# A fifth weight chunk's products ordered by hand among the gates and the first tile of a chunked recurrence

## What is computed

```python
proj = einsum("bsd,de->bse", rms_norm(x, attn_norm), w_in)        # 1024 x 4104
q_a, k_a, v_a, g_a, beta_a, alpha_a, q_b, k_b, v_b, g_b = split(proj)
# a: gated delta rule, 4 heads of 128, after a causal convolution of q_a, k_a, v_a and silu
beta = sigmoid(beta_a);  g = -exp(a_log) * softplus(alpha_a + dt_bias);  gc = cumsum(g)
# per chunk of tokens: (I + A) u = rhs is solved, then
v_new = u - w @ state;  o = q_dec @ state + attn @ v_new;  state = state * last + k_dec^T @ v_new
# b: retention, 4 heads of 128, rotary q and k, the same kind of state recurrence
x = x + concat(o_a, o_b) @ w_out
x = x + top-2 mixture of 64 experts(rms_norm(x, ffn_norm))
return rms_norm(x, final_norm)
```

## Time and profile before

| | |
|---|---|
| median of three runs | 2205.02 us |
| the profiled execution's own time | 2204.05 us |
| its span, first to last instruction | 2202.3 us |
| what lies around the span | 1.75 us |
| busy shares of the span: PE, DVE, ACT, POOL | 88%, 37%, 28%, 23% |
| mean granted TensorE clock | 0.946 of full |

### The profile page before, as it was taken

How to read it: one execution, slowest core, us unless ns; L and a number is a source line. 1 busy time by engine, 2 the same in 40 slices (tenths; PEclk the granted TensorE clock), 3 DMA queues, 4 the chain that set the end, 5 groups by cost and what they waited for, 6 DMA issues and landing times. The chain is left out here.

```text
span 2202.3 us, 30297 instructions
## 1 busy us (share of the span) xinstructions
PE 1939.9 (88%) x11659; PEld 1334.3 (61%) x11659; DVE 814.9 (37%) x1457; ACT 622.2 (28%) x1325; POOL 514.4 (23%) x587
## 2 busy tenths in 40 slices
PE   5999999999899989999998589999969887888880
PEld 5998866666687766878887566766633232332220
DVE  5223245555433542440110446766631111111115
ACT  4333145555323442331210333322212111111111
POOL 2235240000120110001111577666311111111103
PEclk9999999999999999999999699999969998999895
DMA  5113461211321154722321512221468999999986
GB/s 191 50 40 123 143 204 25 49 25 44 125 77 39 42 112 68 94 57 94 91 86 59 191 64 92 78 88 54 170 264 360 424 424 425 423 421 420 418 359 241
DMA packets 101711, 371.75 MB, mean 169 GB/s; under 512 B 17413, under 2 KB 40138, under 8 KB 74698
## 3 DMA queue, kind: packets, MB, share of 16 engines
q1 hardware_dynamic: 83722, 323.59, 41.0%
q0 software_dynamic: 16704, 42.10, 4.9%
q10 hardware_dynamic: 1152, 4.19, 0.5%
HBM read 321.47 MB, written 65.14 MB: 176 GB/s over the span
## 5 line engine op out<-in xcount | busy, mean ns | idle before, releaser
L2712 PE MATMUL ps<-w_gu,rows_t 128*64 128x512 f32 x1024 | 263.7, 674 | 62.8 <-DMA w_gu<-w_up 61.1
L2712 PEld LDWEIGHTS ps<-w_gu,rows_t 128*64 128x64 f32 x1024 | 79.9, 154 | 223.5 <-issue 158.3
L930 PE MATMUL ps<-k_s,q_s 96*128 96x512 f32 (+3 forms) x384 | 150.7, 503 | 0.0
L2787 DVE TENSOR_TENSOR act_s<-act_g,ps 128x256 f32<-128x256 f32 x32 | 13.5, 421 | 334.2 <-ACT act_g L2778 334.2
L2970 POOL DMA_INDIRECT y_d<-y_out,asg_i x32 | 32.1, 1004 | 438.0 <-DVE y_out L2796 438.0
L305 PE MATMUL ps<-tk_lo,h_hi 128*128 128x512 f32 x320 | 125.4, 392 | 3.0 <-DVE tk_lo L297 3.0
L305 PE MATMUL ps<-tk_hi,h_lo 128*128 128x512 f32 x320 | 125.1, 391 | 0.0
L305 PE MATMUL ps<-tk_hi,h_hi 128*128 128x512 f32 x320 | 125.1, 391 | 0.0
L2185 PE MATMUL ps<-w_o,mix_t 128*128 128x512 f32 x256 | 124.8, 616 | 0.0
L2730 PE MATMUL ps<-w_d,act_tt 128*64 128x512 f32 x512 | 116.9, 598 | 0.5 <-issue 0.5
L484 PE MATMUL ps<-w_u_lo,x_hi 128*128 128x444 f32 (+2 forms) x256 | 93.7, 366 | 15.4 <-DVE x_lo L297 15.4
(11 more groups left out here) (447 smaller groups left out, 3995.6 us busy)
## 6 DMA issues: line engine op xcount, KB each, us to landing
w_gu<-w_gate SPq DMA_DIRECT2D x64, 1024.0 KB, 22.1
w_gu<-w_up SPq DMA_DIRECT2D x64, 1024.0 KB, 25.5
w_d<-w_down SPq DMA_DIRECT2D x64, 1024.0 KB, 19.0
w_tk<-w_in SPq DMA_DIRECT2D x5, 2048.0 KB, 12.0
proj_d<-tok_o POOLq DMA_DIRECT2D x40, 256.0 KB, 2.3
tk_in<-proj_d SPq DMA_DIRECT2D x8, 1280.0 KB, 6.6
yf<-y_d SPq DMA_DIRECT2D x4, 2048.0 KB, 14.2
w_ch<-w_in SPq DMA_DIRECT2D x12, 512.0 KB, 9.8
```

The costliest lines, as they stand in the source:

```text
L930: mm = pe.matmul(ps[:, b, 0:cn], q_s[p][:, a, i * P:(i + 1) * P], k_s[p][:, a, g * BANK:g * BANK + cn], start=True, stop=True)
L2712: mm = pe.matmul(ps[half, 2, :].rearrange("p (g n) -> p g n", g=2), rows_t[:, k, half], w_gu[q][:, h, :, k, :], start=(k == 0), stop=(k == ...
```

## The change

The fifth chunk leaves section c and is cut into 24 thirds of eight products (k0 to k23; three per token tile). A list `BESIDE` replaces d0 and the steps -1 and 0, and each engine (SP apart) goes through it in its order: PE does the thirds k, the gate sums gc and the n pieces of tile 0; ACT and DVE copy the finished tiles (v0 to v7) between their gate operations and pieces; POOL stores them (w0 to w7). The waits on the phase counter go: the conv stores alone release the first loads, the fourth chunk's last product releases the other begins, and `load_tk` waits for the store of its own tile. Each tile's thirds use banks 3 to 7, 0 to 2 are the n pieces' banks. Buffers are placed anew; those of tile 0 lie outside the chunk's operands. The clearing of both states and of one `u_fin` half moves behind the last product and behind w7. `load_tk` of tile 1 and the load of `w_o2` are issued after the last product; the gains are all done in step 1, two rows where one was.

```diff
-        tk_jobs = Jobs(base, [0, 1, 2, 3, 4, 5, 6, 7], 5)
+        tk_jobs = Jobs(base, [0, 1, 2, 3, 4, 5, 6, 7], 4)
+        t4_jobs = Jobs(base, [3, 4, 5, 6, 7, 3, 4, 5], 1)
+        def conv_over(eng):
+            for p in range(2):
+                wait(eng, s_cst[p], 16 * NCH // 2)
+        def three_chunks_over(eng):
+            wait(eng, bank_full[7], tk_jobs.base[7] + 4)
+        def products_over(eng):
+            wait(eng, bank_full[t4_jobs.banks[T - 1]], t4_jobs.before(T - 1, 0) + 1)
+        def last_product(pe, i):
+            t, third = divmod(i, 3)
+            if i == 0:
+                wait(pe, s_low, TOK + 4)
+            b = job_start(pe, t4_jobs, t, 0) if third == 0 else ps[:, t4_jobs.banks[t], :]
+            toks = slice(t * P, (t + 1) * P)
+            for n in range(KD * third, KD * third + KD):
+                k, part = divmod(n, 3)
+                a, w = ((h_hi, tk_lo[0]), (h_lo, tk_hi[0]), (h_hi, tk_hi[0]))[part]
+                mm = pe.matmul(b, a[:, k, toks], w[:, k, :], start=(n == 0), stop=(n == 3 * KD - 1))
+            if third == 2:
+                job_end(mm, t4_jobs, t)
...
-            for p in range(2):
-                wait(pool, s_cst[p], 16 * NCH // 2)
-            for q in range(4):
-                wait(pool, s_tst[q], 16 * 10)
-            wait(pool, bank_free[4], bt_jobs.base[4] + 1)
-            pool.sem_inc(s_phase, 1)
...
+        BESIDE = ("begin a_sums0 g_begin k0 k1 k2 a_norm0 k3 v0 gc k4 w0 g_end trig0 k5 n_turn k6 k7 v1 n_decay k8 w1 n_scores k9 k10 v2 k11 w2 n_first "
+                  "k12 n_y1 k13 v3 n_ut1 k14 w3 n_y2 k15 n_ut2 v4 k16 n_y3 w4 k17 n_ut3 k18 v5 n_y4 k19 n_ut4 w5 a_sums1 k20 n_y5 k21 v6 n_ut5 "
+                  "a_norm1 trig1 k22 n_y6 w6 k23 n_ut6 v7 w7").split()
...
         def d0_sp(sp):
-            wait(sp, s_phase, PH_C)
+            conv_over(sp)
...
             load_qkv(sp, 0)
-            sp.dma_start(rot[:, :, :], A["c_rot"].rearrange("(t p) n -> p t n", p=P)).then_inc(s_din, 16)
-            load_tk(sp, 0)
             load_qkv(sp, 1)
+            three_chunks_over(sp)
+            sp.dma_start(rot[:, :, :], A["c_rot"].rearrange("(t p) n -> p t n", p=P)).then_inc(s_wr, 16)
...
-            sp.dma_start(w_o2[:, :, :], A["w_out_2"][0].rearrange("(k p) n -> p k n", p=P)).then_inc(s_wo2, 16)
+            load_tk(sp, 0)
+            sp.dma_start(fg_row[:, :], A["ffn_norm_2"][0].partition_broadcast(P)).then_inc(s_fg, 16)
             sp.dma_start(w_r[:, :, 0:GROUPS], A["w_router_group_2"][0].rearrange("(p k) n -> p k n", p=P)).then_inc(s_wr, 16)
             sp.dma_start(w_r[:, :, GROUPS:], A["w_router_expert_2"][0].rearrange("(p k) n -> p k n", p=P)).then_inc(s_wr, 16)
-            sp.dma_start(fg_row[:, :], A["ffn_norm_2"][0].partition_broadcast(P)).then_inc(s_fg, 16)
+            products_over(sp)
             load_tk(sp, 1)
+            sp.dma_start(w_o2[:, :, :], A["w_out_2"][0].rearrange("(k p) n -> p k n", p=P)).then_inc(s_wo2, 16)
         def load_tk(sp, t):
+            wait(sp, s_tst[t % 4], 16 * (9 + t // 4))
...
         def gains(i):
-                    if t > 1:
+                    if t != 1:
                         return
-                    act.activation(w_o2[:, k, :], w_o2[:, k, :], ACT.Copy, scale=gain_ab[:, g:g + 1]).then_inc(s_wos, 1)
+                    for k in (2 * i, 2 * i + 1):
+                        act.activation(w_o2[:, k, :], w_o2[:, k, :], ACT.Copy, scale=gain_ab[:, g:g + 1]).then_inc(s_wos, 1)
...
         def by_table(t, dst, c0, name):
+                if t == 0:
+                    wait(pool, s_wr, 48)
...
+            d_begin(pool, pieces, dict(own, begin=begin_pool, a_sums0=lambda: a_sums(0), a_sums1=lambda: a_sums(1),
+                                       trig0=lambda: trig(0), trig1=lambda: trig(1)))
+            products_over(pool)
+            pool.memset(s_a[:, :, :], 0.0).then_inc(s_zero, 1)
+            pool.memset(s_b[:, :, :], 0.0).then_inc(s_zero, 1)
+            wait(pool, s_zero, 3)
+            pool.memset(u_fin[1][HALVES[1], :, 0:HB], 0.0).then_inc(s_zero, 1)
+            wait(pool, s_zero, 4)
+            d_steps(pool, pieces)
```

More of the change, by code:

```diff
@@ L1499, in chunks @@
             if eng.engine in (mybir.EngineType.PE, mybir.EngineType.SP):
-                for n, place in enumerate((0, 1, 4, 3, 2)):
+                for n, place in enumerate((0, 1, 4, 3, 2)[:5 if eng.engine == mybir.EngineType.SP else 4]):
                     chunk(n, n // 2, n % 2, place * BANK + (2 * AH if n else 0), place * BANK, n in (0, 2))
@@ L1505, in chunks, with last_copied, last_stored @@
                 chunk(2 * i + 1, i, 1, (BANK + 2 * AH) + i * (2 * BANK), BANK + i * (2 * BANK), False)
-            chunk(4, 2, 0, 2 * BANK + 2 * AH, 2 * BANK, False)
+        def conv_over(eng):
[17 more added lines that the diff above has]
+                job_end(mm, t4_jobs, t)
+        def last_copied(eng, t):
+            wait(eng, s_tst[t % 4], 16 * (8 + t // 4))
+            b = job_read(eng, t4_jobs, t, 0)
+            if eng.engine == mybir.EngineType.Activation:
+                ins = eng.activation(tok_o[t % 4][:, :], b, ACT.Copy)
+            else:
+                ins = eng.tensor_copy(tok_o[t % 4][:, :], b)
+            job_done(ins, t4_jobs, t)
+        def last_stored(pool, t):
+            wait(pool, bank_free[t4_jobs.banks[t]], t4_jobs.before(t, 0) + 1)
+            pool.dma_start(proj_d[t * P:(t + 1) * P, C_GATE_A + 2 * BANK:C_GATE_A + 3 * BANK], tok_o[t % 4][:, :]).then_inc(s_tst[t % 4], 16)
         def b_end(pool):
@@ L1981, in d_sp @@
                     copied(sp, "SR", T - 1)
+                    full(sp, "ST", T - 1)
                     load_pair(sp, 1)
@@ L1989, in d_sp, with d0_act @@
             load_pair(sp, 2)
-        def d0_act(act):
+        def d0_act(act, end):
             g3 = lambda i: gs(i).rearrange("p (t h) -> p t h", t=T)
[L1993 to L2000, removed]
+            if not end:
+                wait(act, bank_free[4], bt_jobs.base[4] + 1)
+                act.activation(g3(G_BETA), ba[:, :, 0:AH], ACT.Sigmoid).then_inc(s_gact, 1)
+                act.wait_ge(s_din, 32)
+                act.activation(gates[:, G_EA, 0:AH], gate_rows[:, 0, :], ACT.Exp).then_inc(s_gact, 1)
+                act.wait_ge(s_gdve, 3)
+                act.activation(gs(G_E), gs(G_NX), ACT.Exp, scale=-1.0).then_inc(s_gact, 1)
+                act.wait_ge(s_gdve, 4)
+                act.activation(gs(G_SP), gs(G_E), ACT.Ln).then_inc(s_gact, 1)
+                return
             act.wait_ge(s_gdve, 9)
@@ L2048, in flat4, with d_begin @@
             return ap.rearrange("p h n -> p (h n)")
+        def d_begin(eng, pieces, own):
+            for name in BESIDE:
+                if name in own:
+                    own[name]()
+                elif name in pieces:
+                    pieces[name](0)
         def d_steps(eng, pieces):
-            for s in STEPS:
+            for s in STEPS[2:]:
                 for name in ENDING.get(s, ORDER):
@@ L2226, in d_pe @@
                 pieces[f"e_p{i}"] = lambda t, i=i: project(t, int(i > 1), range(4 * i, 4 * i + 4) if i < 2 else OUT1[i])
+            own = {f"k{i}": lambda i=i: last_product(pe, i) for i in range(3 * T)}
+            d_begin(pe, pieces, dict(own, gc=lambda: d0_pe(pe)))
+            pe.wait_ge(s_zero, 4)
             d_steps(pe, pieces)
@@ L2320, in d_act, with begin_act @@
                 pieces[f"n_ut{i + 2}"] = gains(i)
+            def begin_act():
+                conv_over(act)
+                three_chunks_over(act)
+            own = {f"v{t}": lambda t=t: last_copied(act, t) for t in range(0, T, 2)}
+            d_begin(act, pieces, dict(own, begin=begin_act, g_begin=lambda: d0_act(act, False), g_end=lambda: d0_act(act, True),
+                                      a_sums0=lambda: a_sums(0), a_sums1=lambda: a_sums(1)))
+            products_over(act)
             d_steps(act, pieces)
@@ L2584, in o_sq @@
             def o_sq(t):
+                if t == 0:
+                    for q in range(4):
+                        wait(pool, s_tst[q], 16 * 10)
                 copied(pool, "AV", t)
@@ L3098, in _ @@
             c_pe(pe)
-            d0_pe(pe)
             d_pe(pe)
```

120 lines of the change are left out of this document (67 added, 53 removed).

## The result

The changed kernel took 2174.24 us (median of 4 runs, 2172.23 to 2177.55), the kernel before 2203.51 (4 runs) beside it. The ratio is 0.987, 95% interval 0.9858 to 0.9882. The forecast was 2176.0. The profiled execution took 2172.23 us with a span of 2170.5.

A forecast was written before the change was run, and what follows sets the result against it. PE was taken to idle in the 51.1 us behind the fifth chunk, on the gate chain and small pieces waiting for copies. 2204.05 - 29.9 (merged stretch and handover) + 1.8 (step 1) = 2176.0 us, range 2168 to 2186.

The forecast's parts named there:

- A: Distance from k0 to the first piece of step 1 on PE, 94.75 us before; forecast to run from 1159.8 to 1224.6.
- terms 2 and 3: Merged stretch on PE: tile 0's pieces at full clock, 13.7 us, and 16 returns to the products at 0.15, 2.4 us.
- term 5: Handover to step 1: from k23's end PE waits for the clearing behind v7 and w7, 4.3 us; bounds 3.3 and 5.
- Term 1: Merged stretch: the fifth chunk's 192 products stay at 0.227 us each, 43.5 us.
- Term 4: Gate chain on ACT and DVE, 8.1 us against four thirds' 7.25: PE waits 0.9 us; bounds 0 and 3.
- The first rival: PE stands between the thirds because one late engine holds all; 8.5 us more, 2184.5; chance 0.14.
- (a): Loads in step 1: w_o2 lands at about 1241.5, ACT wants it at 1241.6, so it just fits; cost zero.
- (b): Gains in step 1: eight on ACT instead of four delay the squares of tile 2; +1.8 us, bounds 0 and 4.6.
- (c): Clock entering step 1: 0.5 and back after 5 to 6 us as before, cost 0; staying full gives 1.9 us.
- The slower rival: Clock falls over the merged stretch; at 1.2 GHz throughout the time would be 2236 us; chance 0.03.

The follow-up runs named there:

- Run 2: Changed kernel with, from n_y1 on, two thirds before each n_y and none between it and its n_ut; 2175.15 us (one run).
- run 3: Changed kernel with the clearing of the states put right behind k23, ahead of v7 and w7; 2170.76 us (one run).
- run 4: On top of run 3, PE waits for the clearing only ahead of its first product with a state; 2170.94 us, ratio 0.9853 to the kernel before.
- run 5: Changed kernel with the gains of the odd rows of the output weights left out, four ACT instructions instead of eight; 2175.01 us (one run).
- run 7: Run 4 and run 6 combined: clearing early, PE waiting only at the states, gains one piece later; 2171.07 us (one run).
- run 8: Run 7 with the gate sums one third later on PE, behind k4; 2169.05 us (5 runs), ratio 0.9841 to the kernel before.
- run 10: Same kernel as run 8, timed beside the changed kernel on one chip; 2169.15 us, ratio 0.9849 to the kernel before.
- run 1: Changed kernel with the merge undone: all 24 thirds first, then gates and tile 0; 2188.64 us (4 runs), ratio 0.9933 to the kernel before.
- run 6: Changed kernel with the four pairs of gains one piece later on ACT, behind n_ut3 to n_ut6; 2173.26 us (one run).
- run 9: Changed kernel unaltered, timed again on one chip against the same runs of the kernel before; 2173.25 us, ratio 0.9868.

## Why the prediction was right

**The mechanism and the size.** A was forecast at 64.8 us (1159.8 to 1224.6) and came out at 65.17. Two small misses offset each other in part, 0.6 more in terms 2 and 3 and 0.2 less in term 5.

- *Term 1, products:* 0.227 us each in the merged stretch too, but 0.23 in a third behind a group of 64x64 matmuls.
- *Terms 2 and 3, pieces and returns:* PE reached the end of k23 61.1 us after k0; without the products' 43.5 and the wait's 0.85 this leaves 16.75 us, where pieces without `n_ut6` and returns had 16.1. The return was put at 0.15 for all 16, with 0.16 as upper bound, from a row with other products. It is not one size. Around a group of 64x64 matmuls it measures 0.2, outside that bound; around a piece of 128x128 matmuls next to nothing. The timeline of PE in the changed kernel, around `n_turn`:

```profile
1170.38 0.39 PE L1527 MATMUL ps<-tk_hi,h_hi 128*128 128x512 f32 x1
1170.62 1.03 PE L2125 MATMUL ps<-consts,qk_n 128*128 128x128 f32 x8
1171.40 0.48 PE L1527 MATMUL ps<-tk_lo,h_hi 128*128 128x512 f32 x1
1171.72 0.40 PE L1527 MATMUL ps<-tk_hi,h_lo 128*128 128x512 f32 x1
```

  From the first to the last row it is 1.34 us, and the piece's 0.87 with two products of 0.227 make 1.32; around `n_decay` and `n_scores` it comes out alike. The twelve returns around small groups make the forecast 2.4 us by themselves: that term came out right by luck, from fewer returns at a higher price. The 0.6 us are the gate sums (0.7 with their return, where 0.5 stood), some 0.3 for the products at 0.23, and rounding.
- *Term 4, the gate chain:* wait 0.85, forecast 0.9. The table load, by the timeline of ACT in the changed kernel:

```profile
1160.96 1.28 ACT L2042 ACT_TABLE_LOAD   x1
1162.25 0.23 ACT L2042 ACTIVATE gates<-ba 128x32 f32<-128x32 f32 x1
...
1164.13 1.28 ACT L2048 ACT_TABLE_LOAD   x1
1165.43 0.23 ACT L2048 ACTIVATE gates<-gates 128x32 f32<-128x32 f32 x1
```

  A switch costs 1.29 to 1.30 us from start to start, as in the earlier trace rows. The drain that the Trainium skill counts on top ("ScalarE: Activation LUTs", section "What ACT_TABLE_LOAD costs") does not show here either; with it the forecast would have been 2180.
- *Term 5, the handover:* from the end of k23 (1219.02 + 0.23) to 1223.32 it is 4.07 us, forecast 4.3. Its chain in the timeline of the changed kernel is the one that was foreseen: DVE's copy of v7 behind that of `n_ut6`, then POOL's store, then the clearing.

```profile
1220.05 0.42 DVE L2434 TENSOR_SCALAR u_fin<-ps 64x256 f32<-64x256 f32 x1 [3.31 <-PE ps L2189]
1220.39 0.67 DVE L1537 COPY tok_o<-ps 128x512 f32<-128x512 f32 x1
...
1221.37 0.54 POOL L1542 DMA_DIRECT2D proj_d<-tok_o  x1 [7.91 <-DVE tok_o L1537]
1221.90 0.54 POOL L2700 MEMSET s_a<- 128x512 f32 x1
1222.36 0.54 POOL L2701 MEMSET s_b<- 128x512 f32 x1
1222.96 0.31 POOL L2703 MEMSET u_fin<- 64x256 f32 x1
```

**Where a piece could have waited.** The slack held everywhere: no wait of PE but the one for the gates. Run 2 shows that this hangs on the one third behind each `n_y`. The first rival, PE standing between the thirds, did not come; even with all the cover of the `n_ut`s gone it would have been 1.9 us.

**Step 1, (a) the weights.** "It just fits" was right. By the DMA view `w_o2` landed 18.2 us after its issue (19.3 in the earlier trace rows):

```profile
w_o<-w_out SPq DMA_DIRECT2D x1, 4096.0 KB, 18.2
```

Issued at 1219.82, that is 1238.0, and ACT's first gain starts at 1239.68: 1.7 us of slack. In runs 3 and 4, where step 1 starts sooner, it is used up.

**Step 1, (b) the gains.** This is the term that was mis-sized: forecast +1.8 us, measured 0.8 (table in run 5). The step that failed is "the squares of tile 2 start 1.8 later, because gains now end at 25.6 us into the step". The timeline of ACT in the changed kernel:

```profile
1239.68 2.19 ACT L2353 ACTIVATE w_o<-w_o,gain_ab 128x1024 f32<-128x1024 f32 x2
1241.76 0.38 ACT L2322 ACTIVATE y_w<-ps 128x256 f32<-128x256 f32 x1
...
1247.11 0.30 ACT L2298 ACTIVATE sin_x<-qkv_in 128x128 f32<-128x128 f32 x1
```

From the first gain to the squares it is 7.43 us, where before it was 6.82 (1278.30 less 1271.48): 0.6 more, and not 1.8. I had passed the delay of the y3 copy on to the next one whole. In fact the y3 copy comes 2.08 us behind the first gain instead of 1.29, but the y4 copy 5.07 instead of 5.06: ACT had stood 2.36 us before that copy for PE, and the extra gains went into this. Behind the squares it is 0.2 more, on POOL (last section). Counted from the start of step 1 the squares start at 23.79 and 23.82 all the same, because the clock gave the 0.6 back.

**Step 1, (c) the clock.** It fell after the handover as forecast, but came back sooner. Two rows of the windows view, the first of the changed kernel, 3.7 us into step 1, the second of the kernel before, 4.5 us into it:

```profile
1227.00:1229.00 2.00, 2.00 (x17) 2.00 (x17) 1.90 (x5) 1.15 (x2) 0.71 (x1) 0.87 1.02 418
```

```profile
1259.00:1261.00 2.00, 2.00 (x15) 2.00 (x14) 1.84 (x4) 1.15 (x2) 0.92 (x1) 0.71 0.03 8
```

The clock was at half from about 1224.1 to 1227.5, and before until about 1260. Step 1 reached its first gain 0.64 us earlier for it (16.36 us into the step against 17.0), and `d_low` on POOL 0.63 earlier. So step 1 is 35.05 - 0.63 + 0.6 + 0.2 = 35.2 us. That it grew by 0.2 and not by the gains' 0.8 is luck: where the clock falls differs between profiles, and in run 5, where it fell 0.8 us sooner, `d_low` comes at 5.44, nearly as before. At full clock it comes at 4.35 (runs 4, 7, 8 and 10), so a full clock is worth 1.25 us up to there, where the prediction had 1.9.

**The slower rival.** The clock did not fall over the merged stretch: 1.00 for 61.75 us, with PE going back and forth over all eight banks. The condition named against it, that PE never stands a microsecond, held. The case that the Trainium skill describes ("TensorE: Matmul & The Clock Gate", section "A second HAM failure mode: psum-queue depth-cycling") did not arise here.

**The sum.** The profiled execution took 3.8 us less than the forecast: 1.6 us of it is step 1 (1.0 the gains, 0.6 the clock), 1.6 scatter ahead of k0, 0.8 behind `n_decay` of tile 2, and the merged stretch gave 0.3 back. So with the same k0 as before the forecast would have been about 2 us too high.

**What stays open.** The parts of run 1's two differences are read from its waits and clock, not each taken away by itself; the 3.5 us put down to the clock are what remains. Whether another order of the list gives more was tried at one place only, the gate sums. And nothing here settles from which stand of PE on the clock falls: the same one left it at 1.00 in run 8 and not in run 10.

## What to carry to other kernels

Lay a chain of small dependent pieces between equal portions of work that needs nothing of it, each as long as one copy with its hops, and then look at the ends of the merged stretch: here its gate wait, its clearing and the transfer behind it held another 4.1 us. Release the loads of the chain by what they truly need first; that alone was half of this gain. And before charging an engine's added work in full, look for the idle time ahead of its next wanted result. Where the clock can fall at different points, read such a cost at the wait that it sets, and not from a distance that has the clock in it.

## What the runs showed of the hardware

- **A stand can cost more than itself, and not each time.** Stands of PE of 0.87, 1.35 and 1.77 us in run 3 left the clock at 1.00. With one of 2.56 us (run 4) and one of 3.31 us (the changed kernel, runs 5, 6 and 9) it was at 0.50 for about 3.4 us, and with the same 3.31 in run 2 for nearly 7. The length doesn't settle it: the 1.35 us of runs 8 and 10, the same kernel, left 1.00 in one and were followed by 3.4 us at 0.50 in the other. There the squares of tile 2 came 0.7 us later. In run 4 the half clock cost 0.9.
- **Who starts first has the way.** POOL's multiplication of `o_cat` by `tk_in` took 2.35 us before and 3.38 after. In the timeline of the changed kernel DVE's product starts 0.05 us ahead of it and takes 1.22:

```profile
1252.01 1.22 DVE L2397 TENSOR_TENSOR qk_n<-qkv_in,stat_d 128x1024 f32<-128x1024 f32 x1
1252.06 3.38 POOL L2671 TENSOR_TENSOR mixed<-o_cat,tk_in 128x1024 f32<-128x1024 f32 x1
```

  and in that of the kernel before POOL starts first, and DVE's takes 3.03:

```profile
1283.23 2.35 POOL L2590 TENSOR_TENSOR mixed<-o_cat,tk_in 128x1024 f32<-128x1024 f32 x1
...
1283.63 3.03 DVE L2329 TENSOR_TENSOR qk_n<-qkv_in,stat_d 128x1024 f32<-128x1024 f32 x1
```

  Whichever comes second ends about when the two would in a row. POOL's product takes 2.35 us in the two kernels with four gains in step 1 (before, run 5) and 3.38 to 3.40 in step 1 of all others. POOL's next instruction is 0.85 shorter there (0.20 instead of 1.05), and what is left is the 0.2 us behind the squares. This agrees with the Trainium skill, "SBUF — State Buffer", section "SBUF: two separate sides", by which the two engines share one pair of ports, held for a whole instruction; no run here takes this apart.
- **A small load behind a big one.** SP was busy 10.80 us with the issue of the expert half of `w_r` before, behind the 4 MB of `w_o2`, and 2.38 us ahead of it; it landed 8.0 us after its issue, where the earlier trace rows has 15.3.
